# Recurrent tiles: the small products issued by turns to four quarters of the array, and the inverse's second four heads kept with the chunks' halves exchanged

## The chip, the cores and the metric

The kernel runs on one core of one Trainium2 chip. The metric is the device time of one execution in microseconds. The kernel before takes 3699.47 us (median of three runs, 3698.89 to 3702.61). TensorE (PE), VectorE (DVE), ScalarE (ACT), GpSimd (POOL) and SyncE (SP) run programs of their own and meet at semaphores. In the profile PEld are TensorE's weight loads, and TensorE's clock has two levels here, 1.2 and 2.4 GHz (0.50 and 1.00 in the rows).

## What is computed

The program is a first block of attention and a second block of two layers. Each layer of the second block has a feed-forward part, a projection, three mixers over 512 tokens (a sparse attention, four RWKV-7 heads, four gated delta heads), an output projection and a second feed-forward part. The change touches the two recurrent mixers alone. Cut to what matters, the reference has

```
def rwkv7_scan(r, w, k, v, a, b):
    def step(S, inp):
        sa = einsum('bhij,bhj->bhi', S, at)
        S = S * wt[:, :, None, :] + sa[..., None] * bt[:, :, None, :] + vt[..., None] * kt[:, :, None, :]
        return S, einsum('bhij,bhj->bhi', S, rt)

def chunk_gated_delta_rule(q, k, v, g, beta):      # chunks of 64 tokens
    lower = where(strict, einsum('bhncd,bhnsd->bhncs', kb, k) * decay, 0.0)
    sol = triangular_solve(eye(C) + lower, rhs, left_side=True, lower=True, unit_diagonal=True)
    u, wk = sol[..., :Dv], sol[..., Dv:]
    def step(S, inp):
        v_new = uc - einsum('bhck,bhkv->bhcv', wc, S)
        o = einsum(..., qc * exp(gc), S) + einsum(..., ac, v_new)
        S = S * exp(g_last) + einsum(..., kc * exp(g_last - gc), v_new)
```

The kernel computes both mixers in the second form: chunks of 64 tokens, for each chunk and head the inverse of a unit lower triangular 64x64 matrix, and a state that goes from chunk to chunk.

## The kernel before

A layer's 512 tokens are four tiles of 128 tokens, `rec_tile` for j = 0 to 3. A tile holds two chunks, the first on partitions 0 to 63 and the second on 64 to 127 (`HALF`), and all eight heads: the four RWKV heads are columns 0 to 255 of a matrix tile, the four delta heads 256 to 511. Each engine has its own `rec_tile`; they name the same steps and meet at semaphores `K(...)`.

A tile on TensorE goes through these steps. Preparation: cumulative sums (L1487 to L1502), transposes into F1 to F4 (L1516, L1517, L1527, L1528, L1536, L1537, L1547) and a product with a mask (L1556). Then 64x64 and 64x128 products of one chunk and one head: RW (L1573, two banks of PSUM, 16 matrices each), N (L1588, two banks), PN (L1598, two banks). The inverse takes five doubling levels. Level k makes `y = N D` (L1612 through `each`, one bank for each group g of four heads, 8 products in each bank), ACT copies the y of each group into Y (L3314), TensorE makes `d = Dt Y` and `dt = Y Dt` (L1612 again), and DVE copies the entries of the level into D (L2628, 128x256 of 512 columns) and Dt (L2634) under a mask. Level 0 is set by DVE in L2614 (twice), L2618 and L2619 (Dt, 128x512). After the levels come x (L1657, L1663), WT (the second loop of 16 products there), ub (L1679), and for each of the two chunks the state: m (L1690), u (L1698), m again (L1708), with DVE's L2649, L2651 and L2654 between them. The output is od (L1722, L1724, L1727) and o (L1738). DVE and ACT (L3342, L3348) normalise it: L2669, L2670, L2671, L2674, a root in POOL's L3583 and L3585, L2677 to L2683.

One product of 64x64 in f32 is two records of MATMUL and two of LDWEIGHTS. A product reads one half of the rows and writes one half of the columns of the array: it uses one quarter. In `each` the two chunks' products follow one another on the two diagonal quarters (first half in, first half out; second half in, second half out):

```
for h in range(4):
    for c in HALF:
        hs = slice(g * 256 + h * 64, g * 256 + h * 64 + 64)
        ins = mm(b[c, o + h * 64:o + (h + 1) * 64], lhs[c, hs], rhs[c, hs], True, True)
```

Each engine runs its own list in program order. Two planners written as generators set it: `mixer_rounds` runs the attention of a layer in rounds and takes the tile steps in between, and `tile_rounds` interleaves, once tile 0 is under way, the solving of tile j with the state and output of tile j-1 and the preparation of tile j+1. PSUM has eight banks, given out in turn by `bank(key, till)`; TensorE waits there until the reader named `till` of the bank's last content is done. With `of=` the bank of another key is taken again. In the kernel before the d of a level takes the bank of y of group 0 and dt takes the bank of y of group 1.

Of the kernel before, what the change touches and what calls it, by code (L numbers as in the profile page):

```python
# [9 lines left out]
I32 = mybir.dt.int32  # L10
# [5 lines left out]
P = 128  # L16
# [427 lines left out]
def build_program(nc, A, out, dbg):  # L444
    ctx = ExitStack()
    with ctx:
# [197 lines left out]
        def heads_of(ap, k):  # L644
            return ap.rearrange("p (h b) n -> p h b n", h=8)

        def level_mask(k, tr):
            m = level(c64(k + 6 * tr), k, 1 - tr)
            return bc(m.unsqueeze(1), [P, 8, 32 // 2 ** k, 2 ** k]).bitcast(I32)
# [84 lines left out]
        def tensor_program(pe):  # L734
# [713 lines left out]
            def rec_tile(l, j, stock):  # L1448
# [112 lines left out]
                for par in range(2):  # L1561
                    if par:
                        yield
                    b, free = bank(K("RW", par), K("RW", par))
                    pe.wait_ge(*free)
                    pe.wait_ge(*at(*K("F1")))
                    pe.wait_ge(*at(*K("F2")))
                    rs = HALF[par]
                    for q in range(2):
                        for n in range(2):  # L1570
                            for e_, c in enumerate(HALF):
                                o = q * 256 + n * P
                                ins = mm(b[c, o:o + P].rearrange("p (c n) -> p c n", c=2),  # L1573
                                         F2[rs, n * 256 + q * P + 64 * e_:n * 256 + q * P + 64 * e_ + 64],
                                         f1v[rs, q, :, c], True, True)
                    ins.then_inc(*S("rw", par))
                yield
                N = get()
                for par in range(2):
                    b, free = bank(K("N", par), K("N", par))  # L1580
                    pe.wait_ge(*free)
                    pe.wait_ge(*at(*K("F4")))
                    pe.wait_ge(*at(*K("F3")))
                    rs = HALF[par]
                    for a, (lhs, rhs) in enumerate(((f1v, F2), (f4v, F3))):
                        for q in range(2):
                            for e_, c in enumerate(HALF):
                                ins = mm(b[c, (2 * a + q) * 64:(2 * a + q + 1) * 64], lhs[rs, q, 1, c],  # L1588
                                         rhs[rs, q * P + 64 * e_:q * P + 64 * e_ + 64], True, True)
                    ins.then_inc(*S("n", par))  # L1590
                yield
                for par in range(2):
                    b, free = bank(K("PN", par), K("PN", par))
                    pe.wait_ge(*free)
                    rs = HALF[par]
                    for q in range(2):
                        for e_, c in enumerate(HALF):
                            ins = mm(b[c, q * P:(q + 1) * P].rearrange("p (c n) -> p c n", c=2),  # L1598
                                     F3[rs, q * P + 64 * e_:q * P + 64 * e_ + 64], f4v[rs, q, :, c], True, True)
                    ins.then_inc(*S("pn", par))  # L1600
# [6 lines left out]
                def each(b, g, lhs, rhs, o=0):  # L1607

                    for h in range(4):
                        for c in HALF:  # L1610
                            hs = slice(g * 256 + h * 64, g * 256 + h * 64 + 64)
                            ins = mm(b[c, o + h * 64:o + (h + 1) * 64], lhs[c, hs], rhs[c, hs], True, True)  # L1612
                    return ins

                yield
                for k in range(1, 6):
                    Yk = get()
                    for g in range(2):
                        b, free = bank(K("y", k, g), K("Y", k, g))
                        pe.wait_ge(*free)  # L1620
# [8 lines left out]
                    b, free = bank(K("d", k), K("D", k, 1), of=K("y", k, 0))  # L1629
                    pe.wait_ge(*free)  # L1630
# [28 lines left out]
                for e_, c in enumerate(HALF):  # L1659
                    b, free = bank(K("wt", e_), K("WT", e_))  # L1660
                    pe.wait_ge(*free)
                    for h in range(8):
                        ins = mm(b[hb(h), (h // 2) * 64:(h // 2 + 1) * 64], KB[c, h * 64:(h + 1) * 64],  # L1663
                                 Dm[c, h * 64:(h + 1) * 64], True, True)
                    ins.then_inc(*S("wt", e_))
# [17 lines left out]
                for e_ in range(2):  # L1683
# [8 lines left out]
                    for par in range(2):  # L1692
                        b = ub[par]
                        pe.wait_ge(*at(*K("ubx", par)))
                        pe.wait_ge(*at(*K("WT", e_)))
                        pe.wait_ge(*(at(*K("M", 0)) if e_ else at("rec", "M", 1, l, j - 1) if j else at("rec", "M0", l)))
                        for q in range(4):
# [2126 lines left out]
```

## Time and profile before

| | |
|---|---|
| median of three runs | 3699.47 us |
| the profiled execution | 3705.42 us, of it span 3703.6 us |
| DVE, ACT, POOL busy in the span | 1938.7, 1497.7 and 1653.4 us |
| the recurrent tiles of layer 1 | 1971 to 2136.8 us of the span |
| the recurrent tiles of layer 2 | 3138 to 3300.8 us of the span |

The stretches of the two layers are read off the timeline: from the first RW product of tile 0 until the first product of the second feed-forward part. TensorE is busy nearly everywhere, as an average; the windows by tile and by part of a tile tell which engine is dense where. A record of TensorE lasts longer than the distance to the next record of the same line, so the pace of a group is its length less one record's length, divided by the number of records less one.

### The profile page before, as it was taken

What the parts mean: (1) busy time and instruction counts of PE and PEld (TensorE: products, weight loads), DVE (VectorE), ACT (ScalarE), POOL (GpSimd) and SP (SyncE); (2) the same over time, 40 slices, a digit from 0 to 9 for tenths busy, and PEclk for the clock granted to TensorE, in tenths of its full rate; (3) what the DMA queues carried; (4) which work ended last, traced back from release to release, by engine and by line L of the source; (5) the groups of instructions that cost most, each with busy time, mean ns of one, the idle gap of its engine ahead of it and who ended that gap; (6) DMA issues with size and microseconds to landing.
All of it is one profiled execution on the core that took longest, in us unless ns stands there. A gap on an engine that the chain in (4) does not pass through costs nothing.

```text
span 3703.6 us, 55820 instructions
## 1 busy us (share of the span) xinstructions
PE 3608.6 (97%) x23122; PEld 2998.2 (81%) x23122; DVE 1938.7 (52%) x3397; ACT 1497.7 (40%) x2673; POOL 1653.4 (45%) x936
## 2 busy tenths in 40 slices
PE   9999999999899999999999999999999999999999
PEld 8877888888788878888767888888888876788887
DVE  2356554344645544552676635543553396655552
ACT  3444333434433343333455343334333455534332
POOL 3114566421266635664322335663666322235664
PEclk9999999999999999999999999999999999999999
DMA  4103332311243234323210034323332320012332
GB/s 129 41 29 97 114 100 66 95 52 35 67 135 100 69 101 128 101 69 89 75 46 2 3 118 123 103 64 120 104 103 75 88 57 24 3 42 90 99 103 97
DMA packets 393405, 291.95 MB, mean 79 GB/s; under 512 B 17056, under 2 KB 355904, under 8 KB 393152
## 3 DMA queue, kind: packets, MB, share of 16 engines
q1 hardware_dynamic: 387728, 284.49, 25.2%
q8 instruction: 183, 3.00, 0.3%
q10 hardware_dynamic: 5136, 2.70, 0.3%
q0 software_dynamic: 288, 1.18, 0.1%
q14 instruction: 70, 0.57, 0.0%
HBM read 286.24 MB, written 2.10 MB: 78 GB/s over the span
## 4 chain that ended last, share of the span: by engine, by line
PE 83%; DVE 10%; ACT 4%; POOL 2%; issue 1%; ACTq 0%; DMA 0%; DVEq 0%; SPq 0%; POOLq 0%
PE ps L823 13%; PE ps L824 13%; PE ps L825 13%; PE ps L1052 4%; PE ps L1053 4%; PE ps L1054 4%; PE ps L955 3%; PE ps L952 3%; PE ps L954 3%; PE ps L1080 2%; PE ps L1612 2%; PE ps L1100 2%; PE ps L1089 1%; PE ps L1162 1%; PE ps L1227 1%
## 5 line engine op out<-in xcount | busy, mean ns | idle before, releaser
L3461 POOL TENSOR_TENSOR wl<-wraw,wh 128x1024 fp32r<-128x1024 f32 (+1 forms) x424 | 1025.7, 2424 | 1555.5 <-ACT wh L2776 1552.1
L823 PE MATMUL ps<-x_T,wh 128*128 128x512 f32 (+1 forms) x2224 | 850.3, 382 | 0.0
L824 PE MATMUL ps<-x_T,wh 128*128 128x512 f32 (+1 forms) x2224 | 849.0, 382 | 0.0
L825 PE MATMUL ps<-x_T,wl 128*128 128x512 f32 (+1 forms) x2224 | 849.0, 382 | 0.0
L2776 ACT ACTIVATE wh<-wraw 128x1024 fp32r<-128x1024 f32 (+1 forms) x424 | 445.8, 1052 | 763.1 <-PE ps L825 489.9
L823 PEld LDWEIGHTS ps<-x_T,wh 128*128 128x128 f32 x2224 | 418.7, 188 | 81.4 <-POOL wl L3461 0.7
L824 PEld LDWEIGHTS ps<-x_T,wh 128*128 128x128 f32 x2224 | 418.6, 188 | 80.5 <-issue 0.5
L825 PEld LDWEIGHTS ps<-x_T,wl 128*128 128x128 f32 x2224 | 418.6, 188 | 80.4
L2060 DVE TENSOR_TENSOR scr<-scr,ps 128x512 f32<-128x512 f32 x132 | 90.6, 686 | 465.8 <-ACT scr L2931 465.8
L1052 PE MATMUL ps<-wh,h_T 128*128 128x512 f32 x672 | 262.4, 390 | 0.2
L1053 PE MATMUL ps<-wl,h_T 128*128 128x512 f32 x672 | 261.5, 389 | 0.0
L1054 PE MATMUL ps<-wh,h_T 128*128 128x512 f32 x672 | 261.5, 389 | 0.0
L3457 POOL TENSOR_TENSOR wl<-arena,wh 128x512 fp32r<-128x512 f32 x126 | 187.9, 1495 | 121.9 <-ACT wh L2773 121.8
L2106 DVE SCALAR_TENSOR_TENSOR x_tm<-ps,x_tm 128x512 f32<-128x512 f32 x224 | 154.9, 691 | 157.1 <-PE ps L955 78.3
L3457 POOL TENSOR_TENSOR wl<-mix,wh 128x512 fp32r<-128x512 f32 x150 | 212.6, 1435 | 8.2 <-ACT wh L2773 8.2
L2067 DVE TENSOR_TENSOR scr<-scr,ps 128x512 f32<-128x512 f32 x96 | 65.8, 686 | 217.1 <-PE ps L825 216.5
L1052 PEld LDWEIGHTS ps<-wh,h_T 128*128 128x128 f32 x672 | 126.1, 188 | 29.9 <-POOL wl L3457 2.6
L1054 PEld LDWEIGHTS ps<-wh,h_T 128*128 128x128 f32 x672 | 126.2, 188 | 26.1
L1053 PEld LDWEIGHTS ps<-wl,h_T 128*128 128x128 f32 x672 | 126.2, 188 | 25.8
L2773 ACT ACTIVATE wh<-mix 128x512 fp32r<-128x512 f32 x150 | 91.8, 624 | 125.0 <-PE ps L825 47.8
L952 PE MATMUL ps<-wh,h_T 128*128 128x512 f32 x352 | 138.0, 392 | 0.0
L955 PE MATMUL ps<-wh,h_T 128*128 128x512 f32 x352 | 137.1, 390 | 0.0
(822 smaller groups left out, 6876.7 us busy)
## 6 DMA issues: line engine op xcount, KB each, us to landing
wraw<-in_ffn_w_gate_dram SPq DMA_DIRECT2D x88, 512.0 KB, 3.9
wraw<-in_ffn_w_up_dram SPq DMA_DIRECT2D x88, 512.0 KB, 3.9
wraw<-in_w_in_dram SPq DMA_DIRECT2D x82, 512.0 KB, 3.7
wraw<-in_w_gate_dram SPq DMA_DIRECT2D x44, 512.0 KB, 3.9
wraw<-in_w_up_dram SPq DMA_DIRECT2D x44, 512.0 KB, 3.9
mix<-in_ffn_w_down_dram SPq DMA_DIRECT2D x20, 1024.0 KB, 6.8
arena<-in_ffn_w_down_dram SPq DMA_DIRECT2D x12, 1024.0 KB, 6.4
wraw<-in_ffn_w_down_dram SPq DMA_DIRECT2D x24, 512.0 KB, 3.7
```

Of the source, the lines that this page charges most:

```text
L823: mm(b[:, t0:t1], wh[:, k, :], xTh[:, k, t0:t1], k == 0, False)
L824: mm(b[:, t0:t1], wh[:, k, :], xTl[:, k, t0:t1], False, False)
L825: ins = mm(b[:, t0:t1], wl[:, k, :], xTh[:, k, t0:t1], False, k == 7)
L952: mm(o, lh(k, j), wh[:, q, :], k == 0, False)
L955: ins = mm(o, ll(k, j), wh[:, q, :], False, k == K - 1 and not apart)
L1052: mm(b[:, :], hF[:, q, 0, m, t], wh[:, u, :], first and q == 0, False)
L1053: mm(b[:, :], hF[:, q, 0, m, t], wl[:, u, :], False, False)
L1054: ins = mm(b[:, :], hF[:, q, 1, m, t], wh[:, u, :], False, q == pairs - 1)
L2106: return stt(xs, b[:, :], -0.5 if minus else 0.5, xs, ALU.mult, ALU.add)
L2776: copy(hl_of(w)[0], raw_of(w)).then_inc(*s.sig("w", "hi", w))
L3457: tt(wl[:, u, :], fast_src(prod, q), wh[:, u, :].bitcast(F32), ALU.subtract).then_inc(*g.sig("w", "lo", w, u))
L3461: tt(wl, raw_of(w), wh.bitcast(F32), ALU.subtract).then_inc(*g.sig("w", "lo", w))
```

## The change

RW, N, PN, the y and d of each level, WT, u and o are issued by turns to four quarters of the array, into two banks that are taken together, with all waits ahead of the first product. For RW, N, PN, u and o the two halves of the rows (`par`) change places with the loop over the matrices; for WT it is the chunk. For the levels, `each` takes both groups at once. So that the second group uses the other two quarters, its Dt and Y are held with the chunks' halves exchanged: y reads its rows straight and writes its columns crossed, d reads crossed and writes straight, dt reads and writes crossed. dt therefore still uses the two diagonal quarters and one bank. d now has two banks (those of the two y), and dt takes a bank of its own turn where it took that of y of group 1. On DVE the copy into D is two copies, one for each group, with semaphores of their own, and the first Dt is one copy of 128x256 and two of 64x256 that cross the halves. ACT's copy of y is unchanged. The two parts of RW are one step of the planner's rounds now, with an empty step behind. Lines shift: RW is L1577, N L1592, PN L1601, `each` L1618, u L1705, o L1747; on DVE L2629 and L2632 (first Dt), L2643 (D), L2648 (Dt).

The diff, cut (N, PN, WT, u and o are turned in the same way as RW):

```diff
-                for par in range(2):
-                    if par:
-                        yield
-                    b, free = bank(K("RW", par), K("RW", par))
-                    pe.wait_ge(*free)
-                    pe.wait_ge(*at(*K("F1")))
-                    pe.wait_ge(*at(*K("F2")))
-                    rs = HALF[par]
-                    for q in range(2):
-                        for n in range(2):
+                def two_banks(name):
+                    both = [bank(K(name, par), K(name, par)) for par in range(2)]
+                    for _, free in both:
+                        pe.wait_ge(*free)
+                    return [b for b, _ in both]
+
+                bs = two_banks("RW")
+                pe.wait_ge(*at(*K("F1")))
+                pe.wait_ge(*at(*K("F2")))
+                for q in range(2):
+                    for n in range(2):
+                        o = q * 256 + n * P
+                        for par, rs in enumerate(HALF):
                             for e_, c in enumerate(HALF):
...
-                def each(b, g, lhs, rhs, o=0):
+                def each(outs, lhs, rhs, rows, cols, done):
                     for h in range(4):
-                        for c in HALF:
-                            hs = slice(g * 256 + h * 64, g * 256 + h * 64 + 64)
-                            ins = mm(b[c, o + h * 64:o + (h + 1) * 64], lhs[c, hs], rhs[c, hs], True, True)
-                    return ins
+                        for e_ in range(2):
+                            for g in range(2):
+                                c, o = HALF[e_ ^ (rows & g)], HALF[e_ ^ (cols & g)]
+                                hs = slice(g * 256 + h * 64, g * 256 + h * 64 + 64)
+                                ins = mm(outs[g][o, h * 64:(h + 1) * 64], lhs[c, hs], rhs[c, hs], True, True)
+                                if h == 3 and e_:
+                                    done(g, ins)
...
+                    ys = [bank(K("y", k, g), K("Y", k, g)) for g in range(2)]
+                    for _, free in ys:
+                        pe.wait_ge(*free)
+                    keep_warm(ys[0][0], 12 if j == 3 and k == 1 else 0)
                     for g in range(2):
-                        b, free = bank(K("y", k, g), K("Y", k, g))
-                        pe.wait_ge(*free)
-                        keep_warm(b, 12 if j == 3 and k == 1 and not g else 0)
                         pe.wait_ge(*at(*K("D", k - 1, g)))
-                        each(b, g, N, Dm).then_inc(*S("y", k, g))
+                    each([b for b, _ in ys], N, Dm, 0, 1, lambda g, ins: ins.then_inc(*S("y", k, g)))
...
-                    b, free = bank(K("d", k), K("D", k, 1), of=K("y", k, 0))
-                    pe.wait_ge(*free)
+                    ds = [bank(K("d", k, g), K("D", k, g), of=K("y", k, g)) for g in range(2)]
                     pe.wait_ge(*at(*K("Dt", k - 1)))
                     for g in range(2):
+                        pe.wait_ge(*ds[g][1])
                         pe.wait_ge(*at(*K("Y", k, g)))
-                        ins = each(b, g, Dt, Yk, 256 * g)
-                    ins.then_inc(*S("d", k))
+                    each([b for b, _ in ds], Dt, Yk, 1, 0, lambda g, ins: ins.then_inc(*S("d", k, g)))
                     if k < 5:
-                        b, free = bank(K("dt", k), K("Dt", k), of=K("y", k, 1))
+                        b, free = bank(K("dt", k), K("Dt", k))
                         pe.wait_ge(*free)
-                        for g in range(2):
-                            ins = each(b, g, Yk, Dt, 256 * g)
-                        ins.then_inc(*S("dt", k))
+                        each((b[:, 0:256], b[:, 256:512]), Yk, Dt, 1, 1, lambda g, ins: ins.then_inc(*S("dt", k)) if g else None)
...
-                v.copy_predicated(h64(Dt, 8), lvm(0, 1, 8).bitcast(I32), h64(N, 8)).then_inc(*S("Dt", 0))
+                v.copy_predicated(v4(Dt[:, 0:256]), lvm(0, 1).bitcast(I32), v4(N[:, 0:256]))
+                for e_, c in enumerate(HALF):
+                    to = HALF[1 - e_]
+                    ins = v.copy_predicated(v4(Dt[to, 256:512]), lvm(0, 1)[c].bitcast(I32), v4(N[c, 256:512]))
+                ins.then_inc(*S("Dt", 0))
...
-                    v.wait_ge(*at(*K("D", k - 1, 1)))
-                    v.wait_ge(*at(*K("d", k)))
-                    v.copy_predicated(heads_of(level(Dm, k, 1), k), level_mask(k, 0),
-                                      heads_of(level(psum_of(*K("d", k))[:, :], k, 1), k)).then_inc(*S("D", k, 1))
-                    v.also(*K("D", k, 0))
+                    for g in range(2):
+                        v.wait_ge(*at(*K("D", k - 1, g)))
+                        v.wait_ge(*at(*K("d", k, g)))
+                        v.copy_predicated(heads_of(level(Dm[:, 256 * g:256 * g + 256], k, 1), 4), level_mask(k, 0, 4),
+                                          heads_of(level(psum_of(*K("d", k, g))[:, 0:256], k, 1), 4)).then_inc(*S("D", k, g))
```

On TensorE, level 3 of tile 1 in layer 1, before: y of the two groups (ps0, ps1), d into ps0, dt into ps1, then the transposes of tile 2 (L1516, L1517).

```order
L1612 MATMUL ps0<-scr,spare 64x64 [waits dve_rec]
L1612 MATMUL ps0<-scr,spare 64x64 x7
L1612 MATMUL ps1<-scr,spare 64x64 [waits dve_rec]
L1612 MATMUL ps1<-scr,spare 64x64 x7
L1612 MATMUL ps0<-spare,arena 64x64 [waits act_rec]
L1612 MATMUL ps0<-spare,arena 64x64 x7
L1612 MATMUL ps0<-spare,arena 64x64 [waits act_rec]
L1612 MATMUL ps0<-spare,arena 64x64 x7
L1612 MATMUL ps1<-arena,spare 64x64 x16
L1516 MATMUL ps5<-cr,scr 128x128 [waits dve_rec]
L1517 MATMUL ps5<-cr,arena 128x128
```

And in the change, from the last products of the same d: d alternates between ps6 and ps7, and dt goes to ps0, whose last content was tile 2's cumulative sum (L1496), last read by DVE's L2559.

```order
L1618 MATMUL ps7<-spare,arena 64x64
L1618 MATMUL ps6<-spare,arena 64x64
L1618 MATMUL ps7<-spare,arena 64x64
L1618 MATMUL ps0<-arena,spare 64x64 [waits dve_rec]
L1618 MATMUL ps0<-arena,spare 64x64 x15
L1516 MATMUL ps3<-cr,scr 128x128
L1517 MATMUL ps3<-cr,arena 128x128
```

So dt has a wait of its own there, ahead of the transposes.

On DVE, the first two levels of tile 1 in layer 1 in the change: level 0 (L2624 to L2632), then the state step of tile 0 (L2663, L2665) and the copies of level 1, the two of D from ps3 and ps4 and that of Dt from ps3 again.

```order
L2624 COPY_PREDICATED scr<-cr,spare 128x2x64 [waits act_rec,dve_step]
L2624 COPY_PREDICATED scr<-cr,spare 128x2x64
L2628 COPY_PREDICATED scr<-cr,spare 128x256
L2629 COPY_PREDICATED arena<-cr,spare 128x256
L2632 COPY_PREDICATED arena<-cr,spare 64x256 x2
L2657 SCALAR_TENSOR_TENSOR scr<-spare,arena 128x256 [waits pool_rec]
L2518 TENSOR_TENSOR spare<-ps5,pbuf 128x256 [waits pe_rec,dve_rec]
L2522 TENSOR_TENSOR spare<-ps6,pbuf 128x256 [waits pe_rec]
L2663 TENSOR_TENSOR arena<-arena,small 128x256
L2665 TENSOR_SCALAR arena<-ps1 64x256 [waits pe_rec,dve_step]
L2643 COPY_PREDICATED scr<-cr,ps3 128x64x2 [waits pe_rec]
L2643 COPY_PREDICATED scr<-cr,ps4 128x64x2 [waits pe_rec]
```

The same levels before: one copy of D from ps7 and one of Dt from ps0, two banks for both.

```order
L2628 COPY_PREDICATED scr<-cr,ps7 128x128x2 [waits pe_rec]
L2634 COPY_PREDICATED arena<-cr,ps0 128x128x2 [waits pe_rec]
L2529 TENSOR_TENSOR arena<-arena,pbuf 128x256 [waits act_rec]
L2530 TENSOR_TENSOR scr<-arena 128x256 [waits dve_step]
L2628 COPY_PREDICATED scr<-cr,ps7 128x64x4 [waits pe_rec]
L2634 COPY_PREDICATED arena<-cr,ps0 128x64x4 [waits pe_rec]
```

The Dt copy of level 1 now reads from ps3, the bank that the first copy of D has just read, so dt can only be made behind that copy.

## Rows read from the trace of the kernel before

**Rows 1.** The page: TensorE's, VectorE's and the others' busy time.
```profile
PE 3608.6 (97%) x23122; PEld 2998.2 (81%) x23122; DVE 1938.7 (52%) x3397; ACT 1497.7 (40%) x2673; POOL 1653.4 (45%) x936
```

**Rows 2.** Windows by tile: stretch and length, busy us (records), clock, DMA.
```profile
2024.70:2062.70 38.00, 34.21 (x834) 30.83 (x835) 27.43 (x63) 18.38 (x47) 13.22 (x14) 0.96 0.01 3
...
3138.00:3151.70 13.70, 13.09 (x143) 9.12 (x143) 8.00 (x28) 8.02 (x26) 0.00 (x0) 1.00 0.01 2
3151.70:3190.10 38.40, 35.33 (x692) 30.25 (x692) 23.69 (x62) 21.83 (x56) 12.04 (x13) 1.00 0.01 2
3190.10:3226.80 36.70, 33.05 (x836) 29.62 (x837) 28.54 (x66) 17.73 (x46) 13.23 (x14) 1.00 0.01 3
...
3263.40:3300.80 37.40, 32.83 (x905) 31.04 (x905) 19.99 (x41) 10.21 (x26) 5.15 (x6) 0.93 0.01 3
```

**Rows 3.** Windows, one period of layer 2 (tile 1 solving) in three of its four parts.
```profile
3190.10:3205.70 15.60, 15.03 (x341) 12.97 (x341) 10.42 (x27) 5.80 (x15) 3.29 (x3) 1.00 0.01 4
3205.70:3213.50 7.80, 7.44 (x213) 6.89 (x209) 7.41 (x19) 4.96 (x17) 0.46 (x1) 1.00 0.01 2
...
3215.70:3226.80 11.10, 8.41 (x226) 7.80 (x227) 10.69 (x21) 6.10 (x13) 7.52 (x9) 1.00 0.01 3
```

**Rows 4.** Waits of TensorE, same period: us in total, times, longest.
```profile
PE ps L1547 <- POOL spare L3529: 1.8, 1, 1.8
```

**Rows 5.** Timeline of TensorE, layer 1, before and in tile 0: start, us, group.
```profile
1975.70 1.09 PE L1573 MATMUL ps<-wraw 64*64 64x128 f32 x16
...
1978.16 0.45 PE L1588 MATMUL ps<-wraw 64*64 64x64 f32 x8
...
1980.51 0.68 PE L1598 MATMUL ps<-spare,wraw 64*64 64x128 f32 x16
...
2003.38 1.15 PE L1612 MATMUL ps<-spare 64*64 64x64 f32 x32
```

**Rows 6.** Lines by form, mean ns of one: TensorE's records in layer 2.
```profile
L1573 PE MATMUL ps<-wraw 64*64 64x128 f32 x64 | 3.8, 275 | 0.0
L1612 PE MATMUL ps<-wraw,scr 64*64 64x64 f32 x256 | 9.3, 219 | 0.8 <-DVE wraw L2628 0.6 <-DVE wraw L2614 0.2
```

**Rows 7.** Timeline of DVE, layer 2: level 0 of tile 2.
```profile
3226.31 0.30 DVE L2614 COPY_PREDICATED arena<-cr,scr 128x128 f32<-128x128 int32 x1
3226.51 0.44 DVE L2618 COPY_PREDICATED arena<-cr,spare 128x256 f32<-128x256 int32 x1
3226.85 0.75 DVE L2619 COPY_PREDICATED wraw<-cr,spare 128x512 f32<-128x512 int32 x1
```

**Rows 8.** Timeline, layer 2: level 3 of tile 1, and what follows.
```profile
3209.37 1.10 PE L1612 MATMUL ps<-arena,spare 64*64 64x64 f32 x32
...
3210.70 0.15 DVE L2559 COPY small<-ps 128x4 f32<-128x4 f32 x1
...
3211.68 0.42 DVE L2634 COPY_PREDICATED arena<-cr,ps 128x256 f32<-128x256 int32 x1
...
3212.80 0.69 DVE L2674 TENSOR_REDUCE small<-wraw 128x8 f32<-128x512 f32 x1
...
3215.68 1.13 DVE L2677 TENSOR_TENSOR wraw<-wraw,small 128x512 f32<-128x512 f32 x1 [2.19 <-POOL small L3585]
```

**Rows 9.** Windows of layer 1 with the clock at its lower level.
```profile
2053.10:2056.50 3.40, 3.40 (x59) 3.40 (x58) 3.07 (x6) 1.04 (x4) 2.85 (x4) 0.50 0.00 0
...
2131.60:2138.40 6.80, 6.24 (x100) 5.87 (x101) 2.52 (x6) 0.60 (x1) 0.00 (x0) 0.50 0.01 2
```

**Rows 10.** Waits of TensorE, layer 2, tile 0 (3151.7 to 3190.1).
```profile
PE ps L1496 <- ACT arena L3243: 0.9, 1, 0.9
PE ps L1516 <- DVE arena L2549: 0.8, 1, 0.8
```

**Rows 11.** Waits of TensorE, layer 2, last tile (3263.4 to 3300.8).
```profile
PE ps L1708 <- DVE arena L2651: 1.9, 2, 1.2
PE ps L1657 <- DVE wraw L2628: 1.0, 1, 1.0
```

More of the change, by code:

```diff
@@ L1574, in rec_tile @@
                                          F2[rs, n * 256 + q * P + 64 * e_:n * 256 + q * P + 64 * e_ + 64],
                                          f1v[rs, q, :, c], True, True)
-                    ins.then_inc(*S("rw", par))
+                            if q and n:
+                                ins.then_inc(*S("rw", par))
+                yield
                 yield
                 N = get()
-                for par in range(2):
-                    b, free = bank(K("N", par), K("N", par))
-                    pe.wait_ge(*free)
[L1582 to L1586, printed above, removed]
+                bs = two_banks("N")
@@ L1587, in rec_tile @@
+                pe.wait_ge(*at(*K("F4")))
+                pe.wait_ge(*at(*K("F3")))
+                for a, (lhs, rhs) in enumerate(((f1v, F2), (f4v, F3))):
+                    for q in range(2):
+                        for par, rs in enumerate(HALF):
                             for e_, c in enumerate(HALF):
-                                ins = mm(b[c, (2 * a + q) * 64:(2 * a + q + 1) * 64], lhs[rs, q, 1, c],
+                                ins = mm(bs[par][c, (2 * a + q) * 64:(2 * a + q + 1) * 64], lhs[rs, q, 1, c],
@@ L1589, in rec_tile @@
                                          rhs[rs, q * P + 64 * e_:q * P + 64 * e_ + 64], True, True)
-                    ins.then_inc(*S("n", par))
+                            if a and q:
+                                ins.then_inc(*S("n", par))
                 yield
-                for par in range(2):
-                    b, free = bank(K("PN", par), K("PN", par))
-                    pe.wait_ge(*free)
-                    rs = HALF[par]
-                    for q in range(2):
+                bs = two_banks("PN")
@@ L1597, in rec_tile @@
+                for q in range(2):
+                    for par, rs in enumerate(HALF):
                         for e_, c in enumerate(HALF):
-                            ins = mm(b[c, q * P:(q + 1) * P].rearrange("p (c n) -> p c n", c=2),
+                            ins = mm(bs[par][c, q * P:(q + 1) * P].rearrange("p (c n) -> p c n", c=2),
                                      F3[rs, q * P + 64 * e_:q * P + 64 * e_ + 64], f4v[rs, q, :, c], True, True)
-                    ins.then_inc(*S("pn", par))
+                        if q:
+                            ins.then_inc(*S("pn", par))
@@ L1658, in rec_tile @@
                 ins.then_inc(*S("x"))
-                for e_, c in enumerate(HALF):
-                    b, free = bank(K("wt", e_), K("WT", e_))
+                bs = [bank(K("wt", e_), K("WT", e_)) for e_ in range(2)]
+                for _, free in bs:
                     pe.wait_ge(*free)
[L1662 to L1665, printed above, removed]
+                for q in range(4):
+                    for e_, c in enumerate(HALF):
+                        for h in (2 * q, 2 * q + 1):
+                            ins = mm(bs[e_][0][hb(h), q * 64:(q + 1) * 64], KB[c, h * 64:(h + 1) * 64],
+                                     Dm[c, h * 64:(h + 1) * 64], True, True)
+                        if q == 3:
+                            ins.then_inc(*S("wt", e_))
                 if j == 3:
@@ L1728, in rec_tile @@
                 ins.then_inc(*S("od"))
-                for par in range(2):
-                    b, free = bank(K("o", par), K("Yo", par))
+                bs = [bank(K("o", par), K("Yo", par)) for par in range(2)]
+                for _, free in bs:
                     pe.wait_ge(*free)
-                    for q in range(4):
+                for q in range(4):
+                    for par in range(2):
                         for e_, c in enumerate(HALF):
@@ L2633, in rec_tile @@
                         v.wait_ge(*at(*K("dt", k)))
-                        v.copy_predicated(heads_of(level(Dt, k, 0), k), level_mask(k, 1),
-                                          heads_of(level(psum_of(*K("dt", k))[:, :], k, 0), k)).then_inc(*S("Dt", k))
+                        v.copy_predicated(heads_of(level(Dt, k, 0), 8), level_mask(k, 1, 8),
+                                          heads_of(level(psum_of(*K("dt", k))[:, :], k, 0), 8)).then_inc(*S("Dt", k))
                     stock.put(v, l, Yk)
```

37 lines of the change are left out of this document (18 added, 19 removed).

## Prediction

> **What bounds the kernel now.** I read the page first, then windows by tile, then windows inside one tile, then the waits, and the timeline for the pace of the products. The page says TensorE is busy 97% of the span, DVE 52% [rows 1]: on that view every nanosecond taken off TensorE would count. The average hides the recurrent tiles, the only place that is touched. There TensorE has 33.05 of 36.70 us in a middle tile, and DVE 28.54 [rows 2]. Cut inside that tile, the two change places. In the first part TensorE is dense (15.03 of 15.60) and DVE has room (10.42). In the second both are full (7.44 and 7.41 of 7.80). In the last, DVE has 10.69 of 11.10 and TensorE 8.41 [rows 3]. Between the second and the last lie 2.2 us in which DVE waits 2.19 us for POOL's L3585 [rows 8]; TensorE's longest wait of the period, 1.8 us, is for POOL as well [rows 4]. So 21.1 of 36.7 us per period are set by DVE or POOL, and a shorter product passes only in the other 15.6. Ahead of tile 0, between rounds of attention, TensorE has 13.09 of 13.70 us, DVE 8.00 [rows 2]: there it binds.
>
> **What the products can give at most.** On two diagonal quarters 32 records of y take 1.15 us [rows 5]; one lasts 0.22 [rows 6], so one follows the other by (1.15 - 0.22)/31 = 30 ns. RW's 64x128 records: (1.09 - 0.275)/15 = 54 ns [rows 5, 6]. PN shows what four quarters do: it is two groups of eight records on different halves of the rows, and its 16 take 0.68 us, (0.68 - 0.275)/15 = 27 ns for the same size of record, exactly half [rows 5]. I therefore take half for all that goes to four quarters: 15 ns saved for each interval of a 64x64 record, 27 for a 64x128 one. In a tile, y and d are 32 records each on every one of five levels: 10 x 31 x 15 ns = 4.65 us. RW 32 x 27 = 0.86. N, WT and o have 32 records, each of two u 16, by the same 15 ns; that is at most 0.47, 0.47, 0.47 and 2 x 0.24, and as their two banks overlap a little at the seam already I take 0.3 + 0.35 + 0.4 + 0.5 = 1.55. dt stays on two quarters and PN is already there: 0. Together 7.1 us a tile, 57 us for eight tiles, 1.5%. That is the upper end.
>
> The Trainium skill speaks against it in "TensorE: Matmul & The Clock Gate", Part 3: a weight load overlaps matmuls in flight only when its row group differs. Neighbours of the change's order often share their rows. By that rule the pace would stay at 30 ns and the 57 us would be 0, which is rival three. This trace does not agree: eight records of N that all use one half of the rows take 0.45 us, (0.45 - 0.22)/7 = 33 ns [rows 5, 6], about the diagonal pair's 30.
>
> **What the change adds.** (a) DVE's D copy, 0.43 us [rows 8], becomes two of half the size; by a copy of 128x128, 0.30 us with the next starting 0.20 later [rows 7], two end after 0.20 + 0.30 = 0.50, so +0.08 a level. (b) The first Dt, 0.75 us, becomes a 128x256 copy and two on 64 partitions; a 128x256 copy takes 0.44 with the next 0.34 later [rows 7]; I give a 64-partition copy the same, since no row shows one: 0.34 + 0.34 + 0.44 = 1.12, +0.37 a tile (between -0.1, if half the partitions take half, and +0.37). It is hidden: it stands at the start of the part in which DVE has 5 us of room, and nothing before d of level 1 reads it. (c) dt at level 3 of tiles 1 and 2 has a wait on the bank of the next tile's cumulative sum, which DVE's L2559 frees at 3210.70 + 0.15; today that dt starts at 3209.37 [rows 8]. It would start near 3210.95 and end 1.1 later, so the Dt copy moves from 3211.68 to about 3212.1: +0.44, and with it L2674, POOL and L2677, since the transposes behind dt on TensorE and the DVE steps behind the Dt copy queue there: +0.46 in each of four periods. (d) dt at level 1 of tiles 1 and 2 waits for the first D copy, as it sits in that bank: roughly one copy and its semaphores, 0.6 to 0.7 us, ahead of m of the state. That eats what d of level 1 saved (0.46) and I book it so. (e) d now needs both Y copies ahead of its first product, where the first half began behind the first copy; where no other step fills in, a level gains 0.2 instead of 0.9.
>
> **The sum, stretch by stretch.** Ahead of tile 0: RW 0.86 and one drain of about 0.1, N 0.3, all on the path, -1.2 a layer. Tile 0 (with tile 1's RW and N): 5.8 us are saved, but it runs in the rounds of attention, whose own steps TensorE waits for, and behind DVE and ACT, 0.9 and 0.8 us [rows 10], with DVE dense again at its end; I let 0.75 pass in layer 2 and 1.3 in layer 1, where part of it runs at the lower clock. Middle tiles, first part: y, u, d, o by 15 ns are about 2.4 us; (d), (e) and the links of the state (DVE's L2651 and L2654) leave 0.76. The second part, with DVE full, gives nothing, (c) costs 0.46, and three D copies of (a) in dense parts 0.24: -0.06 a period in layer 2. In layer 1 the periods are 38.0 instead of 36.7 us with the same records, because the clock drops to 0.50 for 3.4 us in each [rows 2, 9], just where the next tile's RW and a level's products run; TensorE is wholly busy there (3.40 of 3.40) and these lines are what changes. RW's 0.86 counts nearly in full there, so another 0.95: -1.0 a period. Last tile (no preparation beside it, DVE 19.99 of 37.40 [rows 2]): up to its output norm 1.5 of the 3.7 us saved, since the state's chain through DVE goes on; level 5 0.4, WT 0.2 (TensorE waits there for DVE 1.0 and 1.9 anyway [rows 11]), two u 0.5, o 0.6 at the lower clock [rows 9]: -3.2.
>
> Layer 1: -1.2 - 1.3 - 2 x 1.0 - 3.2 = -7.7. Layer 2: -1.2 - 0.75 - 2 x 0.06 - 3.2 = -5.3. Together -13.0 us. The profiled execution, 3705.4 us, would be 3692.4; it is 6 us above the median of the runs, so the median goes from 3699.5 to **3686.5 us**.
>
> **The rivals.** One: more passes. The parts that I call set by DVE have TensorE full too (7.44 of 7.80), and DVE's start there follows TensorE's; if a shorter y moves ACT's copies, and they DVE, half of the 57 us gets through: 3671. All of it would be 3643, against which the 10.69 of 11.10 speak. Two: it is swallowed. TensorE, finishing sooner, idles longer in front of DVE and POOL, and the clock falls in more places; each such stretch of 3.4 us holds up to 1.7 us of work more than it would take at 1.00 [rows 9]. Four of these in layer 2, which has none in its middle tiles, and 7 of the 13 us are gone: 3693 to 3700. Three, on the other side: the four quarters give nothing, because neighbours with the same rows wait for each other, and only the additions stay: (a) 5 x 0.08 and (b) 0.37 on each of eight tiles, 6.2 us, (c) 4 x 0.46 = 1.8, (d) 4 x 0.65 = 2.6, together 10.6: **3710**. It turns to the other side once the pace of y is above about 27 ns: the gross gain of 15.8 us (13.0 + 4 x 0.46 + 4 x 0.24) is proportional to the 15 ns, and with 2.7 of them left it is the 2.8 that (c) and (a) take off. If neighbours even doubled their pace it would be 57 us more, 3757. Against both stand PN's 27 ns and N's 33 ns. Four: the change does not do what it says, in that the two groups' products still come out one behind the other because the bank waits, all ahead of the first product now, hold the whole group until the later of two D or Y copies; then y and d gain what they lose at their start, only RW, N, WT, u and o are left, 2.4 of 7.1 us a tile, and a third of 15.8 less 2.8 is -2.5: 3697, inside rival two's range.
>
> The skill's "TensorEngine Tiling (Array Packing)", Gotcha 1, says that different row tiles cannot access one PSUM bank at once. The change gives the row halves two banks wherever it turns them. PN's two groups in this trace are in two banks as well, and no run here shows one bank.
>
> **How the numbers follow.** My forecast, 3678 to 3692, has 0.44; more passing (rival one) 0.18; swallowed to within 0.2% of no change (two and four) 0.28; slower (three) 0.10. What a measurement of this kernel can tell from no change is about 0.2%, 7.4 us: faster means below 3692, slower above 3707. So faster 0.62, same 0.28, slower 0.10. For 8 in 10 I leave out the far half of rival one (below 3668, about 0.10) and nearly all of three: 3668 to 3704. The forecast's own range is 3678 to 3692.
>
> **What would show it.** Right: 32 records of y and d in 0.6 to 0.7 us, RW's in 0.6; dt still 1.1; the window ahead of tile 0 shorter by 1.2 and the last tile by 3; middle tiles of layer 2 within half a microsecond of 36.7; DVE's share of their last part unchanged. In the middle tiles dt of level 3 starts behind L2559 and dt of level 1 behind the first D copy. Wrong: y's records still 30 ns apart (rival three), or the middle tiles of layer 2 shorter by over 1.5 us (rival one: then TensorE, not DVE, set them), or stretches of 0.50 in layer 2's middle tiles (rival two).

## The result and the profile after

The changed kernel takes 3709.46 us (median of 15 executions, 3702.84 to 3715.24) against 3700.89 us for the kernel before (15 executions, 3698.54 to 3708.48). The ratio is 1.0019, with a 95% interval of 1.0013 to 1.0026: slower by about 7 us by that ratio (the two medians are 8.6 us apart), where 13 us less were forecast, and outside the range given. The profiled execution is the shortest of the 15 (3702.84 us, span 3701.0), 6.6 us under their median, so it is read for the order of events and for single places, and not for the sum.

The first step of the prediction holds. The timeline of TensorE in layer 1, ahead of and in tile 0 (start, us, group):

```profile
1969.72 1.10 PE L1577 MATMUL ps<-wraw 64*64 64x128 f32 x32
...
1979.80 0.69 PE L1618 MATMUL ps<-spare 64*64 64x64 f32 x32 [0.98 <-DVE spare L2628]
```

RW's 32 records now take what 16 took [rows 5], (1.10 - 0.27)/31 = 27 ns from one to the next, and y's 32 take 0.69 us, (0.69 - 0.22)/31 = 15 ns. The pace is half of what it was, as the prediction said. For u the section on the change is not exact: all its products for one chunk write the same half of the columns, so they come by turns to two quarters, where they used one and then the other before. Its 16 records take 0.68 us, (0.68 - 0.22)/15 = 31 ns, although they go to two banks; two banks alone do not give the 15 ns.

```profile
3269.81 0.68 PE L1705 MATMUL ps<-arena,spare 64*64 64x64 f32 x16
```

What came of the pace shows in the windows of the page's columns by tile (from the first y of one tile to the first y of the next; layer 1 tiles 1 and 2, then layer 2 ahead of tile 0, and its tiles 0 to 3):

```profile
2016.30:2053.90 37.60, 29.98 (x832) 26.34 (x832) 28.07 (x70) 17.14 (x46) 13.24 (x14) 0.91 0.01 3
2053.90:2091.60 37.70, 30.99 (x833) 26.77 (x833) 28.15 (x70) 14.55 (x41) 12.60 (x13) 0.91 0.01 3
3132.50:3146.20 13.70, 12.72 (x155) 8.76 (x155) 8.58 (x31) 8.88 (x29) 0.00 (x0) 1.00 0.01 2
3146.20:3186.40 40.20, 33.09 (x690) 27.10 (x691) 24.57 (x69) 21.83 (x57) 12.05 (x13) 0.92 0.01 2
3186.40:3224.20 37.80, 29.23 (x838) 25.27 (x839) 29.52 (x73) 17.45 (x46) 13.25 (x14) 0.95 0.01 3
3224.20:3262.30 38.10, 31.18 (x838) 27.55 (x839) 29.44 (x73) 14.57 (x41) 12.61 (x13) 0.91 0.01 3
3262.30:3298.70 36.40, 28.53 (x904) 26.46 (x904) 20.20 (x46) 9.70 (x26) 5.16 (x6) 0.91 0.01 4
```

Tile 1 of layer 2 has 29.23 us of busy TensorE where it had 33.05, but lasts 37.80 us where it lasted 36.70 [rows 2]. TensorE stands idle for 8.6 us in it instead of 3.7, and the clock, 1.00 before in every tile of that layer but the last, is 0.91 to 0.95 in all of them. DVE has 1 us more.

Where TensorE stands idle the list of its waits tells, for a stretch that takes in the wait ahead of that tile's first y (3183.6 to 3221.1; us in total, times, longest):

```profile
PE ps L1618 <- DVE scr L2628: 1.7, 1, 1.7
PE ps L1618 <- DVE small L2569: 1.7, 1, 1.7
PE ps L1547 <- POOL spare L3543: 1.6, 1, 1.6
PE ps L1705 <- DVE arena L2668: 1.2, 1, 1.2
PE ps L1601 <- DVE spare L2593: 0.7, 1, 0.7
PE ps L1618 <- ACT spare L3328: 0.6, 1, 0.6
PE ps L1618 <- DVE scr L2643: 0.6, 1, 0.6
```

The wait for POOL was there [rows 4]. The first row is y of level 1. Before, it began at 3190.09, 0.65 us after the start of L2614's copies (3189.44); now it begins at 3186.40, 0.99 us after the start of the same copies (3185.41), since it waits for L2628, the copy of the second group, as well. The rest of the 1.7 us is TensorE being there sooner. DVE and TensorE, before and then in the change:

```profile
3189.44 0.51 DVE L2614 COPY_PREDICATED scr<-cr,spare 128x128 f32<-128x128 int32 x2
...
3190.09 1.15 PE L1612 MATMUL ps<-scr,spare 64*64 64x64 f32 x32 [0.61 <-DVE scr L2614]
```

```profile
3185.41 0.51 DVE L2624 COPY_PREDICATED scr<-cr,spare 128x128 f32<-128x128 int32 x2
3185.82 0.44 DVE L2628 COPY_PREDICATED scr<-cr,spare 128x256 f32<-128x256 int32 x1
...
3186.40 0.69 PE L1618 MATMUL ps<-scr,spare 64*64 64x64 f32 x32 [1.73 <-DVE scr L2628]
```

The second row is the wait of dt at level 3 for the bank that L2569 reads (L2559 before), which the prediction named. Of the rows of 0.6, one is d of level 3 that waits for both groups' Y copies, and the last is dt of level 1 that waits for the bank of the first D copy, the prediction's (d). One place shows most of it. Level 3 of tile 1 in layer 2, on TensorE and then on DVE:

```profile
3203.91 0.69 PE L1618 MATMUL ps<-spare,arena 64*64 64x64 f32 x32 [0.63 <-ACT spare L3328]
3206.29 1.97 PE L1618 MATMUL ps<-arena,spare 64*64 64x64 f32 x32 [1.69 <-DVE small L2569]
3208.20 0.47 PE L1516 MATMUL ps<-cr,scr 128*128 128x128 f32 x1
```

```profile
3206.09 0.15 DVE L2569 COPY small<-ps 128x4 f32<-128x4 f32 x1
...
3208.32 0.43 DVE L2648 COPY_PREDICATED arena<-cr,ps 128x256 f32<-128x256 int32 x1 [1.10 <-PE ps L1618]
...
3209.81 0.69 DVE L2688 TENSOR_REDUCE small<-wraw 128x8 f32<-128x512 f32 x1
```

```profile
3202.85:3206.26 3.41, 1.13 (x57) 0.88 (x48) 3.22 (x9) 3.07 (x13) 0.00 (x0) 1.00 0.02 5
3206.27:3209.67 3.40, 3.38 (x39) 3.26 (x40) 1.99 (x6) 0.42 (x2) 0.00 (x0) 0.50 0.00 0
```

(The last fence is windows again.) d waits 0.63 us for the second Y copy, dt 1.69 us for its bank, and TensorE is busy 1.13 of 3.41 us. Then the clock falls to 0.50, just as it has work: dt takes 1.97 us where it took 1.10 [rows 8], the transposes 0.42 to 0.47 each, and DVE waits 1.10 us for dt. From the start of L2569 to the start of L2688 it is 3.72 us; before it was 3210.70 to 3212.80, 2.10 us [rows 8]. The step that was booked at +0.46 is +1.6 here.

It is so in this one of the four periods only. In the other three dt waits as long, but runs at the full clock, and the same piece of DVE takes 2.54 us: 2037.04 to 2039.58, 2074.68 to 2077.22, and in tile 2 of layer 2 (TensorE, then DVE):

```profile
3245.55 1.15 PE L1618 MATMUL ps<-wraw,scr 64*64 64x64 f32 x32 [1.68 <-DVE small L2569]
```

```profile
3245.34 0.15 DVE L2569 COPY small<-ps 128x4 f32<-128x4 f32 x1
...
3247.88 0.69 DVE L2688 TENSOR_REDUCE small<-spare 128x8 f32<-128x512 f32 x1
```

That is +0.44, the size that the prediction gave. The lower clock, where it falls on this place, costs the other 1.18 us.

A level of tile 0 in which nothing else is ready shows where the faster y and d went. The kernel before had y, d and dt of such a level in one piece, and the changed kernel has a hole:

```profile
3161.92 3.14 PE L1612 MATMUL ps<-spare 64*64 64x64 f32 x96
```

```profile
3158.30 0.69 PE L1618 MATMUL ps<-spare 64*64 64x64 f32 x32
3159.05 0.45 ACT L3328 ACTIVATE spare<-ps 128x128 f32<-128x128 f32 x2 [2.19 <-PE ps L1618]
...
3159.64 1.62 PE L1618 MATMUL ps<-spare 64*64 64x64 f32 x64 [0.64 <-ACT spare L3328]
```

From the start of y to the end of dt it is 3.14 us before and 3159.64 + 1.62 - 3158.30 = 2.96 us after. Of 2 x 0.46 us saved on TensorE 0.18 is left, since both Y copies now follow the whole y, and d needs both.

### The profile page after: what moved, and what is told of

Read it like the earlier page. It is cut to its first block, busy times and chain, and to the rows that moved or that the text cites. A ratio compares the mean times of both kernels' runs of the same rounds, so it can differ in the third digit from the quotient of the medians.

```text
span 3701.0 us, 55942 instructions
## 1 busy us (share of the span) xinstructions
PE 3574.2 (97%) x23122; PEld 2959.9 (80%) x23122; DVE 1946.1 (53%) x3453; ACT 1494.7 (40%) x2673; POOL 1653.9 (45%) x936
## 3 DMA queue, kind: packets, MB, share of 16 engines
q0 software_dynamic: 288, 1.18, 0.1%
## 4 chain that ended last, share of the span: by engine, by line
PE 83%; DVE 10%; ACT 4%; POOL 1%; issue 1%; ACTq 0%; DMA 0%; DVEq 0%; SPq 0%; POOLq 0%
PE ps L823 13%; PE ps L824 13%; PE ps L825 13%; PE ps L1052 4%; PE ps L1053 4%; PE ps L1054 4%; PE ps L955 3%; PE ps L952 3%; PE ps L954 3%; PE ps L1080 2%; PE ps L1100 2%; PE ps L1618 1%; PE ps L1089 1%; PE ps L1162 1%; PE ps L850 1%
```

## The experiments

**How the clock is read.** Each execution has a mean granted clock c. With two levels, 1.00 and 0.50, the span spends 2 x (1 - c) of its length at the lower one. In the mean that is 63 us for the kernel before and 101 us for the changed one. Within one kernel, executions with more of it are longer: 0.20 to 0.23 us for each us in the executions of the kernel before (15 to 35 in a set), 0.24 in the 15 of the changed kernel, and 0.19 to 0.50 in the smaller sets of the other kernels. All runs, with ratios to the kernel before on the same chip, and the mean time at the lower clock:

| run | what | ratio, 95% interval | lower clock, us |
|---|---|---|---|
| before | | 1 | 63 |
| changed | | 1.0019 [1.0013, 1.0026] | 101 |
| e1 | two quarters at a time in y and d, same waits | 1.0011 [1.0002, 1.0020] | 77 |
| e2 | RW, N, PN, WT, u, o alone | 0.9991 [0.9982, 1.0000] | 66 |
| e3 | levels alone | 1.0042 [1.0030, 1.0055] | 104 |
| e4 | changed, with unread products | 1.0007 [0.9998, 1.0015] | 86 |
| e5 | changed, dt in other banks | 1.0005 [0.9996, 1.0014] | 93 |
| e6 | e5 with unread products | 0.9998 [0.9989, 1.0006] | 80 |
| e7 | e2 with unread products | 0.9982 [0.9974, 0.9991] | 50 |
| e8 | e5, group by group, waits by group | 0.9986 [0.9977, 0.9994] | 73 |
| e9 | e5, two quarters at a time, joint waits | 1.0003 [0.9994, 1.0012] | 84 |
| e10 | e8 with unread products | 0.9985 [0.9977, 0.9994] | 59 |
| e11 | before, with unread products | 1.0012 [1.0003, 1.0021] | 59 |
| e12 | e5 for level 3 alone | 1.0009 [1.0000, 1.0018] | 103 |

A difference of two of these ratios is uncertain by about 0.1%, 4 us; where less is said to differ, it is said so.

**e1 to e4: the parts, and the idle time.** Theory A was the clock: TensorE, done sooner, stands idle longer in one piece, and its clock falls. Rival B was the added waits and the DVE copies alone.

e1 turns one loop:

```diff
                 def each(outs, lhs, rhs, rows, cols, done):
-                    for h in range(4):
-                        for e_ in range(2):
-                            for g in range(2):
+                    for g in range(2):
+                        for h in range(4):
+                            for e_ in range(2):
```

> The changed kernel with one loop order altered: in the levels, the 16 products of y (and of d) go group by group, so two quarters work at a time as before; banks, waits, DVE copies and all other products stay as changed. Theory A (the quarters save the time, but TensorE then stands idle longer in one piece and its clock falls to the lower level in more places): y's 32 records take 1.1 to 1.2 us again, the time at the lower clock falls from 90.6 us of the changed kernel's profile towards the 62.0 of before, and the time stays within 5 us of the changed kernel, 3704 to 3712. Rival B (the clock does not matter; the waits on banks and the longer DVE copies eat the gain): the saved work of y and d comes back on top of them, 3714 to 3722.

Ratio 1.0011: with y and d slower again the kernel is not slower but, if anything, faster, at 77 us of lower clock for 101. The test is weaker than it was meant to be: y's 32 records take 0.98 us here, and not 1.1 to 1.2, so it gives back 0.29 of the 0.46 us. That part of the pace is worth nothing in this kernel, which B as it stood excluded.

e2 takes the code of the levels from the kernel before, e3 all but the levels:

```diff
 e2
-                    each([b for b, _ in ys], N, Dm, 0, 1, ...)
+                        each(b, g, N, Dm).then_inc(*S("y", k, g))
 e3
-                bs = two_banks("RW")
+                for par in range(2):
+                    b, free = bank(K("RW", par), K("RW", par))
```

> Only RW, N, PN, WT, u and o by turns on four quarters; the levels (y, d, dt, DVE's copies, the banks) as before. Theory A: about 2.4 us a tile are saved, no wait is added, the idle stretches grow little: time at the lower clock 55 to 75 us, 3692 to 3701. Rival B: nothing of what B blames is left, 3690 to 3694.

> Only the levels as changed; RW, N, PN, WT, u and o as before. Theory A: the long idle stretches ahead of y of level 1 and of dt of level 3 are there, so the lower clock is too: over 75 us of it, 3703 to 3712. Rival B: as the changed kernel without its best part, 3710 to 3716.

e2 is faster, 0.9991, at the lower clock of before; e3 is the slowest of all, 1.0042, above what both theories gave. The harm sits in the levels. The other products are worth 0.09% alone and 0.23% beside the changed levels; why more there, no run shows. e3 stands 0.23% above the changed kernel with the same time at the lower clock (104 and 101 us), so that time alone does not set the difference between two kernels.

e4 fills the waits with products of an identity that nobody reads:

```diff
-                    keep_warm(ys[0][0], 12 if j == 3 and k == 1 else 0)
+                    keep_warm(ys[0][0], 12 if j and k == 1 else 0)
...
                 b, free = bank(K("F2"), K("F2"))
                 pe.wait_ge(*free)
+                keep_warm(b, 10 if j > 1 else 0)
```

> The changed kernel, with products whose result nobody reads put where TensorE waits longest: 12 of 128x384 ahead of y of level 1 in tiles 1, 2 and 3 (in the changed kernel in tile 3 alone) and 10 ahead of the transposes that wait for POOL in tiles 2 and 3. Theory A: the lower clock in the tiles falls from 47.7 us to under 25, and the time to 3694 to 3703. Rival B: nothing is gained, and where the products run past the end of the wait 0 to 3 us are lost: 3709 to 3713.

Ratio 1.0007, 15 us less at the lower clock: the direction of A, by less than A said. In its profile three stretches at the lower clock (from about 2044, 2082 and 3249 us) begin within 1 us of the end of the wait for dt's bank, which e4 does not fill.

**e5 and e12: dt's bank.**

```diff
-                        b, free = bank(K("dt", k), K("Dt", k))
+                        other = (("rec", "la", l, j + 1) if k == 1 and j in (1, 2) else
+                                 ("rec", "o", 1, l, j - 1) if k == 3 and j else None)
+                        b, free = bank(K("dt", k), K("Dt", k), of=other)
```

> The changed kernel with dt in other banks: at level 1 of tiles 1 and 2 that of the next tile's second preparation product, at level 3 of tiles 1 to 3 that of the second half of the output of the tile before, both read long before. So the two waits that the change put ahead of dt (for the first copy of D, and for L2559) are gone, all else stays. Theory B (those waits set the loss): 1.7 us of idle TensorE ahead of dt of level 3 vanish, middle tiles shorten by 0.5 to 1 us each, time 0.10 to 0.20% under the changed kernel, 3698 to 3703 against 3703 of before. Theory A (the lower clock sets it): 0.05 to 0.15% too, by the stretches at the lower clock behind that wait alone. Rival C (neither: DVE's two copies for each level and the waits on both Y set it): the gap goes but the time stays within 0.05% of the changed kernel.

> e5 with the level-3 half alone: dt of level 3 (tiles 1 to 3) in the bank of the second half of the output before, dt of level 1 left in the bank of D's first copy. The prediction put the level-3 wait at 0.46 us in each of four periods (1.8 us, 0.05%) and the level-1 wait at no net cost; e5 gained 0.14% by taking both away. If the level-3 wait is the larger one (1.7 us of idle TensorE ahead of it), most of that stays: ratio to before 1.0005 to 1.0011. If it is the level-1 wait, which also holds up the state's m, the ratio stays at 1.0013 to 1.0019.

e5 gives 1.0005, 0.14% under the changed kernel, inside the ranges of both B and A; e12, without the bank of level 1, 1.0009. So the two waits cost about 5 us, and the level-3 wait, by these ratios, the larger part, 0.10 of 0.14%. e5's difference is just clear of its uncertainty, e12's is not. A dt that takes another key's bank also takes none from the turn, so the banks of the steps behind it shift; what that does was not tested by itself. In e5's timeline the same piece of DVE, from that copy (L2571 there) to the reduction (L2690), is back at 2.16 us in all four periods, here in tile 1 of layer 2:

```profile
3203.05 0.15 DVE L2571 COPY small<-ps 128x4 f32<-128x4 f32 x1
...
3204.09 0.42 DVE L2650 COPY_PREDICATED arena<-cr,ps 128x256 f32<-128x256 int32 x1
...
3205.21 0.69 DVE L2690 TENSOR_REDUCE small<-wraw 128x8 f32<-128x512 f32 x1
```

**e8 and e9: the joint waits.** e9 is e5 with e1's loop. e8 also gives each group its own waits again, just ahead of its half:

```diff
+                    def d_ahead(g):
+                        pe.wait_ge(*ds[g][1])
+                        pe.wait_ge(*at(*K("Y", k, g)))
-                    for g in range(2):
-                        pe.wait_ge(*ds[g][1])
-                        pe.wait_ge(*at(*K("Y", k, g)))
-                    each([b for b, _ in ds], Dt, Yk, 1, 0, ...)
+                    each([b for b, _ in ds], Dt, Yk, 1, 0, ..., d_ahead)
```

> As e5, but the products of a level go group by group (two quarters at a time), and each group waits for its own bank, its own D and its own Y only, as before the change. Left of the change of the levels are then the two DVE copies a level, the three for the first Dt and the crossed halves. Rival C: these still cost 0.1 to 0.2% over e2, ratio to before 1.000 to 1.001. Theory B: next to nothing is left, ratio to before as e2's, 0.999. Theory A: few long idle pieces, under 25 us at the lower clock in the tiles, ratio 0.998 to 1.000.

> e5 (dt in other banks) with the products of y and d two quarters at a time, but still with both groups' waits ahead of the first product: it stands between e5 and e8. If the joint waits are what costs (Rival C), it is 0.1 to 0.2% slower than e8, ratio to before 0.9995 to 1.0010. If what e5 lost against e8 is the lower clock that idle time brings (Theory A), the slower pace fills the idle time: ratio to before 0.9985 to 1.0000 and 70 to 85 us at the lower clock where e5 has 93.

e9 is 1.0003, e8 0.9986: the joint waits cost 0.17%, 6 us, clear of the uncertainty. Nothing else differs between the two, though each was measured beside the kernel before on a chip of its own. e5, which has the pace of four quarters over e9 (0.69 for 0.97 us of y) and the same waits, is at 1.0005: the pace gives nothing, twice now. e8 keeps DVE's two copies of D and three of the first Dt and is no slower than e2, so Rival C's part on DVE is not seen; its part on the waits is. e8's windows of tiles 0, 1 and 2 of layer 2:

```profile
3147.60:3185.60 38.00, 32.38 (x692) 27.17 (x693) 24.72 (x69) 21.78 (x56) 12.04 (x13) 1.00 0.01 2
3185.60:3221.20 35.60, 29.84 (x836) 25.99 (x837) 29.37 (x73) 17.81 (x46) 13.24 (x14) 1.00 0.01 3
3221.20:3257.10 35.90, 31.72 (x836) 28.13 (x836) 29.34 (x73) 15.37 (x42) 12.59 (x13) 0.95 0.01 3
```

With 29.37 us on DVE, more than before, tile 1 lasts 35.60 us at full clock, 1.1 less than before [rows 2] and 2.2 less than in the changed kernel.

**e6, e7, e10 and e11: the unread products elsewhere.** Each has e4's two edits.

> The run before this one with the unread products of e4 as well, so that every piece of idle time of 1.5 us or more in the middle tiles is filled or gone. Theory A: under 25 us at the lower clock in the tiles, 0.15 to 0.35% under the changed kernel, so faster than before the change. Theory B: as without them, within 0.05%. Rival C: no better than e4.

> e2 (only RW, N, PN, WT, u and o on four quarters, the levels as before) with the unread products ahead of y of level 1 and ahead of the transposes that wait for POOL. Theory A: e2's profile has 7 us at the lower clock in the tiles already, so little is left to win: within 0.1% of e2. Theories B and C: the same as e2 or 1 to 3 us slower.

> e8 (dt in other banks, levels group by group with waits of their own, RW, N, PN, WT, u and o on four quarters) with the unread products of e4. Theory A: 10 to 20 us less at the lower clock than e8's 73 and 0.05 to 0.15% faster than e8: ratio to before 0.997 to 0.998. Otherwise within 0.05% of e8.

> The kernel before, with the unread products of e4 alone, as a control for what they do without the change. Theory A: the kernel before has 63 us at the lower clock in the mean; 10 to 15 less, and 0.05 to 0.1% faster. If they help by something else than the clock, the gain is as large at the same clock.

e11 is the control: on the kernel before they move the lower clock little (59 for 63 us) and cost 0.12%: tiles 0 and 1 of layer 2 last 40.0 and 38.0 us at full clock there, for 38.4 and 36.7 [rows 2]. The gain that A named there did not come. The price may be smaller where the waits are longer, which was not measured by itself. e4, e6 and e7 come out 0.12, 0.07 and 0.09% under their partners (the changed kernel, e5, e2), with 15, 13 and 16 us less at the lower clock. e10 is level with e8 at 14 us less, where A had said 0.05 to 0.15%. e4's difference is at the edge of its uncertainty, those of e6 and e7 are inside it. That three of four go one way while the control goes the other points to a price of the lower clock by itself, and does not prove it. e6 is 0.21% under the changed kernel, inside A's 0.15 to 0.35%, but it is not faster than the kernel before, which A had said as well.

The fastest are e7 (0.9982) and e8 (0.9986), not told apart. Both beat the kernel before and the changed one.

## Why the prediction was wrong

The forecast was -13 us, the result is about +7. In the order of its steps:

- **The pace.** Right: 15 and 27 ns, half for RW, y and d. u's saving is right by luck: 16 records went from 0.92 to 0.68 us, the 0.24 that was booked, but by going from one quarter to two. The rule of the Trainium skill that weight loads overlap only across row groups ("TensorE: Matmul & The Clock Gate", Part 3) would have left 30 ns; the rows with 0.69 and 1.10 us settle that for these shapes, and rival three with it. That rival's 3710 us is the measured median almost to the microsecond, and that is luck: its mechanism did not occur. The prediction also says that no run shows the two row halves in one bank. y of the kernel before does: both chunks of a group write one bank, and records of 0.22 us follow each other at 30 ns [rows 5, 6].
- **Ahead of tile 0.** Nearly right. From the first RW product to the first y it is 10.1 us in both layers (3136.07 to 3146.16 in layer 2) where it was 11.0 (3140.70 to 3151.72): -0.9 of the -1.2. The stretches of 13.70 us do not show it, since they begin ahead of the first RW product.
- **(a) and (b), DVE.** Two D copies span 0.49 us where 0.50 was said. The first Dt takes 1.35 us (3186.16 to 3187.51) where 1.12 was said. No cost of either is seen in the time: e8 has both and is no slower than e2.
- **(c) and (d), the waits of dt.** Right in place, mechanism and size at the full clock: +0.44 in three of four periods, and 0.56 us of idle TensorE ahead of dt of level 1. In the fourth period the clock fell on the very work that DVE waits for, and (c) is +1.6. Together they cost about 5 us by e5, where 1.8 net was booked, a difference that the uncertainty of 4 us covers.
- **(e), the joint waits, and what y and d pass on.** This is the step that failed. The sum let the faster y and d through wherever TensorE was dense, and (e) took a part off only "where no other step fills in", for d and its two Y copies; the wait of y of level 1 for both D copies was put at nothing. y and d are two thirds of the gross 15.8 us (rival four leaves a third without them), some 10.5 us. The runs show none of it (e5 against e9, the changed kernel against e1; both test 0.29 of 0.46 us a y), and e8 against e9 prices the joint waits at 6 us on top. A level of tile 0 kept 0.18 of 0.92 us, and the last tile of layer 2 is 1.0 us shorter in the profile (36.40 for 37.40 [rows 2]) where 3.2 were booked. Rival four named these waits, but let them only cancel the saving: -2.5 us, where the rest alone, e2, gives -3.3.
- **The clock.** The sum moved stretches at the clock that they had, and let the faster products gain at the lower one besides. The clock was an outcome of the change and not a given: 38 us more at the lower clock. At the 0.24 us for each that executions of the changed kernel show, these would be 9 us, an estimate that e3, e11 and e12 do not bear out as a rule between kernels: e12 and e3 have 103 and 104 us of it, the changed kernel 101, and they stand 0.10% below it and 0.23% above it; e11 has less than the kernel before and is slower. Rival two's mechanism, longer idle pieces and stretches of 0.50 in the middle tiles of layer 2, did occur, and its sign of being wrong with it; its range of 3693 to 3700 did not.

Taken one after the other, the runs go from the kernel before to the changed one in four steps: e8 -5.2 us, the joint waits +6.3 (e9), the pace of y and d +0.7 (e5), dt's two waits +5.2 (the changed kernel), together +7.0. That they add up is by construction, since each is the difference of two neighbours; each is uncertain by about 4 us. The clock is inside these steps and not beside them: from e8 to the changed kernel the time at the lower level goes 73, 84, 93, 101 us.

What stays open: how much of each step is the wait and how much the clock that falls behind it. Only one place shows the two apart, (c) at 1.00 and at 0.50. The slope within a kernel is a correlation, and the unread products, which were to settle it, cost time of their own.

## What to carry to other kernels

Faster products pass on only as far as what they wait for is there sooner. If putting two groups into one stream makes the stream wait for the later of two operands, half of that saving, or all, can go into one longer hole, and in this kernel the clock fell behind some of these holes. Before a change takes a buffer by turn, list who read it last and where that reader stands in its own engine's queue: here a copy of 0.15 us, late in DVE's list, held up dt by 1.7 us. Count idle pieces and the clock as results of the change, tile by tile.

## What was not expected of the hardware

At level 3 of tile 1 in layer 2 the clock fell to 0.50 when TensorE had been busy for 1.13 of 3.41 us, in pieces of idle time no longer than 1.69 us. It stayed at 1.00 behind the 1.8 us wait for POOL in the same tile of the kernel before [rows 3, 4], and in the changed kernel's other periods dt ran at the full clock behind the same wait of 1.7 us. Products of two groups that run one behind the other on different pairs of quarters overlap where they meet: 32 records of y in e8 take 0.98 us, where two groups on the same pair took 1.15 [rows 5]. The trace of e8, tile 0 of layer 2:

```profile
3163.71 0.98 PE L1619 MATMUL ps<-spare 64*64 64x64 f32 x32
```
